# A pooling branch with stationary weights and its norm factor moved behind the output projection

## The reference

```python
POOL_WINDOWS = (2, 4, 8, 16)     # four groups of 256 channels
def pool_mixer(u, pool_w, pool_scale):
    ...
    for g, w in enumerate(POOL_WINDOWS):
        ...  # mean over the last w tokens, less u itself
    y = jnp.einsum('bsgc,gcf->bsgf', d, pool_w).reshape(B, S, POOL_WIDTH)
    return y * pool_scale
...
        y_pool = rmsnorm(pool_mixer(u, pool_w[l], pool_scale[l]), pool_out_norm_g[l])
        y_attn = rmsnorm(dilated_attention(...), attn_out_norm_g[l])
        x = x + jnp.concatenate([y_pool, y_attn], axis=-1) @ w_out[l]
```

## Time and profile before

| | us |
|---|---|
| median of 3 runs | 2499.22 (2498.62 to 2500.44) |
| profiled execution | 2498.51 |
| its span | 2496.7 |
| TensorE busy | 2484.4 |
| DVE busy | 1489.8 |
| ACT busy | 1072.9 |
| POOL busy | 113.9 |

### The profile page before, as it was taken

The page is one execution under the profiler, slowest core; times in us unless marked ns, Lnnn a source line. Parts: engine busy times, 40 slices in busy tenths (PEclk is TensorE's granted clock), DMA queues, the critical chain, the costliest instruction groups (busy, mean ns, idle before and its releaser), DMA issues.

```text
span 2496.7 us, 28360 instructions
## 1 busy us (share of the span) xinstructions
PE 2484.4 (100%) x11921; PEld 2060.5 (83%) x11921; DVE 1489.8 (60%) x1271; ACT 1072.9 (43%) x875; POOL 113.9 (5%) x195
## 2 busy tenths in 40 slices
PE   9999999999999999999999999999999999999998
PEld 7888888888888888888878888888888888888887
DVE  5465655544455545778779996644655644456544
ACT  5444443333334334555455544543443433334333
POOL 0000000000000000121110002000000000000000
PEclk9999999999999999999999999999999999999999
DMA  8654676666566756687664457744766656566653
GB/s 302 210 186 137 208 230 206 212 208 199 188 217 221 230 190 213 204 293 215 204 202 151 162 188 238 230 139 147 221 216 213 221 192 196 191 206 232 225 196 135
DMA packets 162174, 510.26 MB, mean 204 GB/s; under 512 B 16656, under 2 KB 45472, under 8 KB 161024
## 3 DMA queue, kind: packets, MB, share of 16 engines
q1 hardware_dynamic: 154976, 486.40, 59.8%
q0 software_dynamic: 6656, 21.52, 2.8%
q10 hardware_dynamic: 416, 0.52, 0.1%
HBM read 466.43 MB, written 4.20 MB: 189 GB/s over the span
## 4 chain that ended last, share of the span: by engine, by line
PE 98%; DVE 1%; ACT 1%; issue 0%; DMA 0%; POOLq 0%; SPq 0%; POOL 0%; ACTq 0%
PE ps L853 31%; PE ps L854 30%; PE ps L857 30%; PE ps L1310 1%; PE ps L1293 1%; DVE weights_lo L1854 0%; DVE conv_out L2135 0%; PE ps L984 0%; PE ps L823 0%; PE ps L1082 0%; PE ps L1055 0%; ACT weights_hi L1369 0%; PE ps L886 0%; PE ps L1227 0%; PE ps L875 0%; PE ps L879 0%
## 5 line engine op out<-in xcount | busy, mean ns | idle before, releaser
L1854 DVE TENSOR_TENSOR weights_lo<-weights_raw,weights_hi 128x2048 fp32r<-128x2048 f32 x431 | 986.8, 2290 | 882.3 <-ACT weights_hi L1369 882.3
L1369 ACT ACTIVATE weights_hi<-weights_raw 128x2048 fp32r<-128x2048 f32 x431 | 825.0, 1915 | 1157.3 <-PE ps L857 1099.5
L853 PE MATMUL ps<-weights_hi,stationary_hi 128*128 128x512 f32 x2408 | 943.8, 392 | 2.2 <-DVE weights_lo L1854 1.1
L854 PE MATMUL ps<-weights_lo,stationary_hi 128*128 128x512 f32 x2408 | 937.3, 389 | 0.0
L857 PE MATMUL ps<-weights_hi,stationary_lo 128*128 128x512 f32 x2408 | 741.6, 389 | 0.0
L853 PEld LDWEIGHTS ps<-weights_hi,stationary_hi 128*128 128x128 f32 x2408 | 452.0, 188 | 97.7 <-issue 3.5
L857 PEld LDWEIGHTS ps<-weights_hi,stationary_lo 128*128 128x128 f32 x2408 | 452.0, 188 | 94.5
L854 PEld LDWEIGHTS ps<-weights_lo,stationary_hi 128*128 128x128 f32 x2408 | 452.2, 188 | 92.4
L853 PE MATMUL ps<-weights_hi,hidden_hi 128*128 128x512 f32 x1008 | 392.1, 389 | 0.0
L854 PE MATMUL ps<-weights_lo,hidden_hi 128*128 128x512 f32 x1008 | 392.1, 389 | 0.0
L857 PE MATMUL ps<-weights_hi,hidden_lo 128*128 128x512 f32 x1008 | 310.2, 389 | 0.0
(11 more groups left out here) (351 smaller groups left out, 959.6 us busy)
## 6 DMA issues: line engine op xcount, KB each, us to landing
weights_raw<-in_w SPq DMA_DIRECT2D x128, 1024.0 KB, 5.5
weights_raw<-in_w_in SPq DMA_DIRECT2D x79, 1024.0 KB, 5.6
weights_raw<-in_w_up SPq DMA_DIRECT2D x64, 1024.0 KB, 5.0
weights_raw<-in_w_down SPq DMA_DIRECT2D x64, 1024.0 KB, 5.7
weights_raw<-in_w_out SPq DMA_DIRECT2D x32, 1024.0 KB, 5.7
hidden<-turned_blocks SPq DMA_DIRECT2D x328, 64.0 KB
weights_raw<-in_wk SPq DMA_DIRECT2D x16, 1024.0 KB, 5.6
weights_raw<-in_wv SPq DMA_DIRECT2D x16, 1024.0 KB, 5.5
```

Of the source, the lines that this page charges most:

```text
L853: pe.matmul(o, xh, WHI[:, slot, j, c * BANK:(c + 1) * BANK], start=first and j == 0, stop=False)
L854: pe.matmul(o, xh, WLO[:, low, j, c * BANK:(c + 1) * BANK], start=False, stop=False)
L1369: act.activation(WHI[:, s % NSPLIT], RAW[:, s % NRAW], ACT.Copy).then_inc(hi_ready, 1)
L1854: dve.tensor_tensor(WLO[:, s % NRAW], RAW[:, s % NRAW], WHI[:, s % NSPLIT].bitcast(F32), ALU.subtract).then_inc(lo_ready, 1)
```

## The change

The averaging's first matmul of each tile is cut to the columns that its window reaches (128 + w instead of 256), and it moves from (1, 0) to (0, 1), between the two token tiles of step 0. The group product takes `pool_w` as the stationary operand and moves from (2, 0) to (1, 0); its result has channels in rows, as the output projection wants it, so there are no transposes. ACT and DVE split it straight from PSUM with `pool_scale` times the norm's gain, one factor for each channel. The norm's factor for each token is not applied to it. ACT also squares the scaled result; DVE adds the squares of the eight tiles as a tree (1024, 512 and 256 columns), and at (2, 1) TensorE sums over the partitions with two matmuls against one column of ones. Each output pass is done as two half passes in separate banks, attention's four steps and pooling's four steps. The first half pass is added onto the residual, the second is multiplied with the norm's factor and added (`add_scaled`). `pool_scale` comes as columns in one early DMA of 4-byte runs, and the wait and the broadcast load that stood in POOL's queue are gone. What the diff leaves out here: the two semaphores' names, `X_PASS[h][half]` in `turn_residual`, and the waits on `tables_landed` at 64 instead of 48.

```diff
--- before.py
+++ after.py
@@ -180,7 +180,9 @@
         PT1 = at("probs_t", [P, 2, NS], A0 + 76)
         ALIBI = at("alibi", [P, 2, NS], A0 + 80)
         BIAS = at("bias", [P, NS], A0 + 83)
-        PSB = at("pool_scale", [P, COLS], A0 + 16)
+        PSQ = at("pooled_squares", [P, HEADS, T], A0 + 0)
+        pool_col = at("pool_scale_columns", [P, HEADS], 114.5)
+        pool_gain = at("pool_scale_and_gain", [P, HEADS], 114.5 + 0.125)
         nmax = small("nmax", [P, 2, 2])
         den = small("den", [P, HEADS, 2])
         rden = small("rden", [P, 2, 2])
@@ -427,7 +429,7 @@
         PS = D // (STEP * P)
         S_IN, P_IN = 0, 0
         S_OUT, P_OUT = S_IN + 4 * PS, P_IN + 4
-        S_MLP, P_MLP = S_OUT + 2 * PS, P_OUT + 2
+        S_MLP, P_MLP = S_OUT + 2 * PS, P_OUT + 4
         HALF_STEPS = 4 * PS + 2 * (HK // STEP)
         HALF_PASSES = 6
         S_IN2, P_IN2 = S_MLP + 2 * HALF_STEPS, P_MLP + 2 * HALF_PASSES
@@ -465,7 +467,7 @@
         for q in range(16):
             if q % 8:
                 RT_AFTER["m", q] = RS_AFTER["m", q] = ("m", q - 1)
-        X_PASS = {H_MLP: P_OUT, H_IN2: P_IN2 - 2, H_XQ: P_OUT2, H_MLP2: P_O}
+        X_PASS = {H_MLP: (P_OUT + 1, P_OUT + 3), H_IN2: (P_IN2 - 2, P_IN2 - 1), H_XQ: (P_OUT2, P_OUT2 + 1), H_MLP2: (P_O, P_O + 1)}
         def blocks_of(name):
             return BLOCKS.get(name, (RT, RS))
@@ -546,7 +548,7 @@
         MEMORY_TILES = [range(0)] * 3 + [range(4), range(4, 6), range(6, 8), range(8, 10), range(10, 12), range(12, 14), range(14, 16)]
-        TURNED = {H_IN: 0, H_OUT: 8, H_OUT2: 16}
+        TURNED = {H_IN: 0, H_OUT: 8, H_OUT2: 12}
         (N_IN, N_ATT, N_POOL, N_MLP, N_F1, N_IN2, N_MEM, N_XQ, N_MLP2, N_F2) = range(NORMS)
         G_IN, G_OUT, G_MLP, G_IN2, G_XQ, G_MEM, G_MLP2, G_F1 = 0, 16, 32, 48, 64, 80, 96, 112
@@ -568,6 +570,9 @@
         def dw_tap(j, c):
             k = j * HEADS + c
             return VEC[:, 2 + k // 124, k % 124:k % 124 + 1]
+        def pooled_tile(m):
+            return ps[:, 4 + m // 2, (m % 2) * T:(m % 2 + 1) * T]
         def blocks(w):
             return w.rearrange("(s j p) n -> s p j n", j=STEP, p=P)
@@ -683,6 +688,7 @@
             pool.dma_start(ALIBI[:], alibi).then_inc(tables_landed, 16)
             pool.dma_start(POOLW[:], pool_w.rearrange("g (c p) f -> p g c f", p=P)).then_inc(tables_landed, 16)
             pool.dma_start(POOLA[:], pool_avg).then_inc(tables_landed, 16)
+            pool.dma_start(pool_col[:], pool_scale.rearrange("(m p) -> p m", p=P), allow_slow_non_contiguous=True).then_inc(tables_landed, 16)
             pool.dma_start(alog[:], a_log.partition_broadcast(P)).then_inc(gates_landed, 16)
             pool.dma_start(dtb[:], dt_bias.partition_broadcast(P)).then_inc(gates_landed, 16)
@@ -705,9 +711,6 @@
             root(N_IN, D)
-            pool.wait_ge(kt_ready, 1)
-            pool.wait_ge(tables_landed, 48)
-            pool.dma_start(PSB[:], pool_scale.partition_broadcast(P)).then_inc(tables_landed, 16)
             root(N_ATT, COLS)
             root(N_POOL, COLS)
             pool.dma_start(BARAW[:], w_in2[:, 4 * COLS:4 * COLS + NBA].rearrange("(k p) n -> p k n", p=P)).then_inc(ba_landed, 16)
@@ -1037,31 +1040,44 @@
             gemm_pass(S_IN + 3 * PS, P_IN + 3, during_u)
             def during_out_a(k, j):
-                if (k, j) == (1, 0):
+                if (k, j) == (0, 1):
                     left(P_IN + 3)
-                    pe.wait_ge(tables_landed, 48)
+                    pe.wait_ge(tables_landed, 64)
                     for n in range(2 * len(WINDOWS)):
-                        for t in range(TT):
-                            last = pe.matmul(ps[:, 4 + n // 2, (n % 2) * T + t * P:(n % 2 + 1) * T], U_ROWS[:, t, n * P:(n + 1) * P],
-                                             POOLA[:, n // 2, t, t * P:], start=t == 0, stop=t == TT - 1)
+                        for t, (c0, c1) in enumerate(((0, P + WINDOWS[n // 2]), (P, T))):
+                            last = pe.matmul(ps[:, 4 + n // 2, (n % 2) * T + c0:(n % 2) * T + c1], U_ROWS[:, t, n * P:(n + 1) * P],
+                                             POOLA[:, n // 2, t, c0:c1], start=t == 0, stop=t == TT - 1, skip_group_check=True)
                     last.then_inc(pooled, 1)
-                elif (k, j) == (2, 0):
+                elif (k, j) == (1, 0):
                     pe.wait_ge(pooled_ready, 1)
-                    pe.wait_ge(tables_landed, 48)
+                    for g in range(len(WINDOWS)):
+                        for f in range(2):
+                            for c in range(2):
+                                last = pe.matmul(ps[:, 4 + g, f * T:(f + 1) * T], POOLW[:, g, c, f * P:(f + 1) * P], DT[:, 2 * g + c, :],
+                                                 start=c == 0, stop=c == 1)
+                        last.then_inc(pool_out, 1)
+                elif (k, j) == (2, 1):
+                    pe.wait_ge(pool_tree, 1)
+                    pe.wait_ge(ht_lo, KT * H_OUT + KT)
                     for t in range(TT):
-                        for g in range(len(WINDOWS)):
-                            for c in range(2):
-                                last = pe.matmul(ps[:, 4 + 2 * t + g // 2, (g % 2) * GROUP:(g % 2 + 1) * GROUP],
-                                                 DT[:, 2 * g + c, t * P:(t + 1) * P], POOLW[:, g, c, :], start=c == 0, stop=c == 1)
+                        last = pe.matmul(ps[:, 4, t:t + 1], PSQ[:, 0, t * P:(t + 1) * P], ONES[:, 0:1], start=True, stop=True)
                     last.then_inc(pool_out, 1)
-                elif (k, j) == (4, 0):
-                    pe.wait_ge(y_ready, 2)
-                    turn8(lambda k, t: U_ROWS[:, t, (k - HEADS) * P:(k - HEADS + 1) * P], 1, 1)
+            def half_pass(s0, p, k0, during=None):
+                for k in range(PS // 2):
+                    if during:
+                        during(k, 0)
+                    step(s0 + k, HHI, HLO, STEP * (k0 + k), p, k == 0, k == PS // 2 - 1,
+                         between=(lambda k=k: during(k, 1)) if during else None)
             pe.wait_ge(ht_lo, KT * H_OUT + KT // 2)
-            gemm_pass(S_OUT, P_OUT, during_out_a, H_OUT)
-            gemm_pass(S_OUT + PS, P_OUT + 1)
+            half_pass(S_OUT, P_OUT, 0, during_out_a)
+            pe.wait_ge(sq_done, TT * (N_POOL + 1))
+            half_pass(S_OUT + PS // 2, P_OUT + 1, PS // 2)
+            half_pass(S_OUT + PS, P_OUT + 2, 0)
+            half_pass(S_OUT + PS + PS // 2, P_OUT + 3, PS // 2)
             mlp(0, S_MLP, P_MLP, H_MLP)
@@ -1499,17 +1515,19 @@
                 for k in range(PS):
                     if n > 0 or k >= AHEAD:
                         split_next(S_OUT + n * PS + k)
-                    if (n, k) == (0, 2):
+                    if (n, k) == (0, 1):
                         act.wait_ge(pooled, 1)
                         act.activation(DT[:].rearrange("p h t -> p (h t)"), ps[:, 4:8, :].rearrange("p b n -> p (b n)"), ACT.Copy).then_inc(pooled_ready, 1)
-                    elif (n, k) == (0, 3):
-
-                        act.wait_ge(y_pool, 1)
-                        for t in range(TT):
-                            act.activation(DT[:, 4 * t:4 * t + 4, :].rearrange("p h t -> p (h t)"), U_ROWS[:, t, :], ACT.Square,
-                                           accum_out=ss[:, TT * N_POOL + t:TT * N_POOL + t + 1]).then_inc(sq_done, 1)
-                    elif (n, k) == (0, 4):
-                        split_turned(H_OUT, lambda k: G_OUT + k, 1, 1)
+                    elif (n, k) == (0, 2):
+                        act.wait_ge(vec_ready, 3)
+                        for g in range(len(WINDOWS)):
+                            act.wait_ge(pool_out, g + 1)
+                            for m in (2 * g, 2 * g + 1):
+                                act.activation(HHI[:, HEADS + m, :], pooled_tile(m), ACT.Copy, scale=pool_gain[:, m:m + 1]).then_inc(ht_hi, 1)
+                            for m in (2 * g, 2 * g + 1):
+                                last = act.activation(PSQ[:, m, :], pooled_tile(m), ACT.Square, scale=pool_col[:, m:m + 1])
+                            last.then_inc(pooled_ready, 1)
                     elif (n, k) == (1, 6):
                         split_blocks(H_MLP, G_MLP, 0)
             ahead(S_MLP)
@@ -2071,22 +2089,37 @@
                 for k in range(PS):
                     if n > 0 or k >= AHEAD:
                         split_next(S_OUT + n * PS + k)
-                    if (n, k) == (0, 3):
-                        dve.wait_ge(pool_out, 1)
+                    if (n, k) == (0, 1):
                         dve.wait_ge(tables_landed, 64)
-                        for t in range(TT):
-                            last = dve.tensor_tensor(U_ROWS[:, t, :], ps[:, 4 + 2 * t:6 + 2 * t, :].rearrange("p b n -> p (b n)"), PSB[:], ALU.mult)
-                        last.then_inc(y_pool, 1)
-                        normalised(N_POOL, U_ROWS)
```

(26 more changed lines are left out.)

## The result

| kernel | us, median (runs) | ratio to the kernel before, 95% interval |
|---|---|---|
| before | 2499.07 (20) | |
| changed | 2502.49, from 2501.01 to 2505.34 (20) | 1.0013, 1.0007 to 1.0019 |

The change makes the kernel 3.4 us slower, 0.13%: within the 0.2% that were called "same", and 2.9 us above the forecast's time of 2499.6. The runs of the changed kernel also spread more, 4.3 us against 2.3. The profiled execution took 2503.45 us, of which the span is 2501.6.

A forecast was written before the change was run, and what follows sets the result against it. TensorE was taken as the bound. Its inserts of 14.76 us become 3.70 + 6.92 + 3.9 + 0.68 = 15.2, so +0.4 on the median gives 2499.6 us; range 2495.4 to 2503.0, own range 2498.8 to 2500.3.

The forecast's parts named there:

- The likeliest case: The forecast itself, given 55%: the pass grows by 0.4 us, TensorE's clock stays at full rate, 2499.6 us.
- the second: Rival given 32%: TensorE's clock drops to half rate in the new wait before the sums, 2501.1 us.
- Averaging, 3.70 us: TensorE's averaging with narrowed first matmuls takes 3.70 us instead of 5.26, scaled by columns between 128- and 256-wide records.
- No wait at the new places: TensorE waits neither before the moved averaging (margin 1.1 us) nor before the moved group product (0.8 us).
- Group product, 6.92 us: With its operands swapped, TensorE's group product stays 32 records of 256 columns, so 6.92 us as before.
- The added wait, 3.9 us: After step 2's first half, TensorE waits 3.9 us for DVE's tree of squares, queued behind a weight split.
- The sums, 0.68 us: TensorE's two one-column matmuls over the squares: 0.44 us for four records plus 0.24 for a slow restart.
- Half passes and scale columns at nothing: Splitting output passes into halves and loading pool_scale as 4-byte columns should cost no time; late weights were given 3%.
- Sum +0.4 us: The first output pass's inserts on TensorE go from 14.76 to 15.2 us, so it grows by 0.4 us.
- The clock falls in the wait: Rival, 32%: TensorE idle before the sums falls to the 1.2 GHz level, losing 1.5 us; result +1.9, 2501.1 us.
- The tail row: Trace row at the kernel's end, cited for the clock rival: clock at 0.51 with TensorE idle some 3.3 us.
- The tree is in time: Rival, 6%: DVE adds the squares before its weight split, the 3.9 us wait vanishes, 3.5 us faster, 2495.7 us.

The follow-up runs named there:

- experiment 4: The changed kernel with the two sums moved half a step later, from (2, 1) to (3, 0): 2496.94 us, ratio 0.9991 to the kernel before.
- experiment 3: The changed kernel with DVE's tree of squares ahead of its split of weights instead of behind it: 2495.40 us, ratio 0.9984 to the kernel before.
- experiment 6: The kernel before with one load added, pool_scale as columns in 1024 runs of 4 bytes: 2499.29 us, ratio 1.0001.
- experiment 2: The changed kernel with 16 unused 512-column matmuls on TensorE ahead of the wait for the tree: 2499.69 us, ratio 1.0002 to the kernel before.
- experiment 8: The changed kernel with two more 2048-column operations on DVE ahead of the tree, lengthening TensorE's wait: 2506.62 us, ratio 1.0031 to the kernel before.
- experiment 1: The changed kernel run again without any edit, beside the kernel before: 2501.68 us, ratio 1.0010.

## Why the prediction was right and where it was off

The forecast of no change beyond 0.2% held, and the time lies in the range. The likeliest case did not come about; the second did. So the range held because it took in that rival: the forecast's own range, 2498.8 to 2500.3, did not hold the time.

- *Averaging, 3.70 us:* 3.67, so the scaling between the 128- and the 256-wide rows held.
- *No wait at the new places:* right for both.
- *Group product, 6.92 us:* 6.92.
- *The added wait, 3.9 us:* 3.99, in both profiles. The DVE timeline of after has the order that the prediction read from the code:

```profile
221.21 0.88 DVE L2099 SCALAR_TENSOR_TENSOR stationary_lo<-ps,pool_scale_and_gain,stationary_hi 128x256 fp32r<-128x256 f32 x2 [0.85 <-ACT pooled_squares L1529]
227.07 2.29 DVE L1872 TENSOR_TENSOR weights_lo<-weights_raw,weights_hi 128x2048 fp32r<-128x2048 f32 x1 [4.98 <-ACT weights_hi L1385]
229.28 2.40 DVE L2104 TENSOR_TENSOR pooled_squares<-pooled_squares 128x1024 f32<-128x1024 f32 x3
```

The last low part is done at 222.1, and the tree starts behind the split only, at 229.28. The additions took 2.40 us together (2.33 from the rows). This was the step with the most links, and it held because each stands in the trace of before with the same neighbours.
- *The sums, 0.68 us:* 0.72 behind a wait at full clock (experiment 4). Without a wait it is 0.48 (experiment 3), so the slow restart that the text added, 0.24, belongs to the wait.
- *Half passes and scale columns at nothing:* no wait stands at a half pass's border, and experiment 6 finds no cost of the columns within what it can tell.
- *Sum +0.4 us:* experiment 2, which has all of this and the clock at 1.00, took +0.6, and the measured inserts make +0.5.

The step that went wrong is the choice between the forecast and the rival *The clock falls in the wait*, which the text gave 32% beside 55% for the forecast; against it stood that the wait is longer than the idle time in the tail "by only 0.6 us". The low clock came in both profiles of the changed kernel, and the lowest of its 31 runs, 2500.67 us, is 1.6 us above the median of before, which suggests that hardly any execution was without it (the profiles show it for two). The rival's term was mis-sized as well: 1.5 us from the kernel's first work, where the two profiles show 3.2 and 1.6, and that of experiment 8 shows 2.2. With +0.5 for the rest, the two medians (+2.6 and +3.4) leave 2.1 and 2.9 us for the clock. The row behind the 1.5 us does not bear it, either. Its six matmuls ran at less than half the usual pace, but the trace of before gives a granted clock of 1.00 for that stretch, so it does not show a low clock:

```profile
2.00:3.00 1.00, 1.00 (x3) 0.77 (x3) 0.00 (x0) 0.71 (x2) 0.00 (x0) 1.00 1.07 280
```

The tail row was the right row. It showed a fall after about 3.3 us, and a wait of 3.9 is longer; that should have made the fall the likeliest case. The Trainium skill ("TensorE: Matmul & The Clock Gate", Part 1: The HAM clock gate) has an idle TensorE go back to half rate and start its next work there. These traces agree in part: 0.50 stands in the stretches behind each idle time of 4 us or more, but in experiment 1 work began again at 1.00, and the level fell 0.4 us into it.

The rival *The tree is in time* was about another order on DVE, and experiment 3 made that order: 2495.40 us against the 2495.7 worked out for it.

## What to carry to other kernels

On a kernel that TensorE bounds, a new wait has two prices: its length, and the clock (it fell behind 4.0 us of idle TensorE, not behind 1.3). The second does not show as idle time, only in the granted clock and in the pace of the matmuls behind it. When a job is put in the middle of another engine's hand-written queue, look what stands ahead of it there: three short additions with their input ready for eight microseconds (221.2 to 229.3) waited behind a split that was itself waiting for TensorE. Moving them up turned a change that cost 2.6 us beside it (3.4 in the first set of runs) into one that gains 3.7.

## What was new about the hardware

- The clock's fall came 3.2, 3.9 and 4.4 us after TensorE's last work (experiment 8, the profile of after, experiment 1), and in the last case 0.4 us after work had begun again. With 1.3 us of idle time it did not fall, nor with 0.4. What sets the delay is open.
- The low clock lasted over 6.8, 3.4 and 4.8 us of work. Two profiles of the same kernel differ by 1.6 us in what it cost, and each length stands in one profile only.
- 1024 runs of 4 bytes took 0.91 us to issue (experiment 6), with no TensorE wait between 28 and 60 us, while they shared the DMA engines with megabytes of weights.
